# Two-layer decoder trunk with mixture-of-experts: Router's work area outside the weight ring, first gathers in the expert block, transposes of the next block at its end

## What is computed

```python
def hier_moe(h, w_rg, b_rg, w_re, b_re, w_gate, w_up, w_down):
    g_top = argmax(xf @ w_rg + b_rg)                 # one of 4 groups
    top_vals, top_idx = lax.top_k(chosen, 2)         # 2 of the 8 experts in it
    weights = p_g[:, None] * softmax(top_vals)
    # every token goes to its 2 of 32 experts:
    #   (silu(x @ w_gate[e]) * (x @ w_up[e])) @ w_down[e], weighted and summed
```

## Time and profile before

| | us |
|---|---|
| median of 3 runs | 1706.45 (1704.6 to 1708.78) |
| the profiled execution, device time | 1702.92 |
| its span, first to last instruction | 1700.7 |
| PE busy / DVE busy / ACT busy / POOL busy in the span | 1543.7 / 689.9 / 298.5 / 44.8 |
| mean granted TensorE clock | 0.968 |
| expert block of layer 0, about | 270 to 758 |
| expert block of layer 1, about | 1185 to 1700 |
| bytes read from HBM | 468.64 MB |

### The profile page before, as it was taken

One profiled execution on the slowest core, in us unless ns is written; L12 is line 12 of the kernel. 1 busy time (PEld: TensorE's weight loads), 2 busy tenths in 40 slices (PEclk: granted clock), 3 DMA queues, 4 the chain that ended last, 5 costly groups with the idle time before them and its releaser, 6 DMA issues. The chain is left out here.

```text
span 1700.7 us, 18753 instructions
## 1 busy us (share of the span) xinstructions
PE 1543.7 (91%) x7356; PEld 719.3 (42%) x7356; DVE 689.9 (41%) x1453; ACT 298.5 (18%) x648; POOL 44.8 (3%) x59
## 2 busy tenths in 40 slices
PE   7999985999998899959999899994999999898994
PEld 3444442444443334435554455552344444333342
DVE  3111353343333333346264587545233333323334
ACT  2000010000100000022243477511000000000001
POOL 0000000000000000000000000000000000000000
PEclk9999997999999999989999999997999999999997
DMA  6261227999999999935310300144999999999992
GB/s 198 74 256 66 78 100 308 420 421 421 421 420 420 422 421 419 419 132 154 98 51 0 149 1 1 19 171 169 418 421 421 419 421 422 421 420 421 420 417 93
DMA packets 109938, 465.28 MB, mean 274 GB/s; under 512 B 26512, under 2 KB 53136, under 8 KB 59920
## 3 DMA queue, kind: packets, MB, share of 16 engines
q1 hardware_dynamic: 104512, 455.56, 66.5%
q0 software_dynamic: 5328, 8.40, 1.4%
HBM read 468.64 MB, written 6.29 MB: 279 GB/s over the span
## 5 line engine op out<-in xcount | busy, mean ns | idle before, releaser
L832 PE MATMUL ps<-raw,e_xT 128*64 128x512 f32 x2080 | 470.9, 600 | 50.8 <-DMA raw<-in_expert_w_up 50.8
L832 PEld LDWEIGHTS ps<-raw,e_xT 128*64 128x64 f32 x2080 | 155.6, 138 | 354.6 <-issue 351.3
L856 PE MATMUL ps<-raw,e_hT 128*64 128x512 f32 x1040 | 237.5, 598 | 1.4
L963 DVE TENSOR_TENSOR e_sg_hid<-e_sg_hid,ps 64x512 f32<-64x512 f32 x65 | 44.2, 681 | 458.6 <-ACT e_sg_hid L905 458.6
L949 DVE TENSOR_TENSOR x_res<-x_res,ps 128x512 f32<-128x512 f32 x264 | 169.1, 682 | 12.2 <-PE ps L870 10.3
L366 PE MATMUL ps<-c_hT,raw 128*128 128x512 f32 x384 | 165.0, 592 | 0.2 <-ACT c_hT L311 0.2
L870 PE MATMUL ps<-e_yhi,e_pick 64*128 64x512 f32 x520 | 111.3, 423 | 13.1 <-issue 5.4
L856 PEld LDWEIGHTS ps<-raw,e_hT 128*64 128x64 f32 x1040 | 68.9, 136 | 128.0 <-issue 111.3
L905 ACT ACTIVATE e_sg_hid<-ps 64x512 f32<-64x512 f32 x65 | 38.6, 595 | 477.0 <-PE ps L832 477.0
L1530 PE MATMUL ps<-a_spare,raw 128*128 128x512 f32 x256 | 114.5, 604 | 1.5 <-DVE a_spare L1321 1.5
L913 ACT ACTIVATE e_yhi<-ps,e_wtab 128x512 fp32r<-128x512 f32 x65 | 44.8, 689 | 395.8 <-PE ps L856 395.8
(11 more groups left out here) (228 smaller groups left out, 1232.1 us busy)
## 6 DMA issues: line engine op xcount, KB each, us to landing
raw<-in_expert_w_gate SPq DMA_DIRECT2D x130, 1024.0 KB, 26.5
raw<-in_expert_w_up SPq DMA_DIRECT2D x130, 1024.0 KB, 27.2
raw<-in_expert_w_down SPq DMA_DIRECT2D x130, 1024.0 KB, 27.0
raw<-in_conv_w_in SPq DMA_DIRECT2D x12, 1024.0 KB, 9.8
raw<-in_w_kv SPq DMA_DIRECT2D x6, 1024.0 KB, 6.2
raw<-in_conv_w_out SPq DMA_DIRECT2D x1, 4096.0 KB, 19.0
rows_x<-raw SPq DMA_DIRECT2D x8, 512.0 KB, 2.7
raw<-in_attn_w_in SPq DMA_DIRECT2D x4, 1024.0 KB, 5.4
```

The source lines that it names most:

```text
L832: mm = pe.matmul(ps_gu[C - C * i:2 * C - C * i, :], xT[:, q % 2, k, u * C:(u + 1) * C], ring(m, L, p)[:, kk * F:(kk + 1) * F], start=(k == ...
L856: mm = pe.matmul(ps_y[n * C:(n + 1) * C, :], hT[:, 2 * h + kk, :], ring(m, L, p)[:, kk * D + n * 512:kk * D + (n + 1) * 512], start=(h == ...
```

## The change

- The ring gets a 17th place, `raw3`, in the expert block's own memory. `NR` is 17; the first 16 places are as before.
- `Router`'s work area no longer lies in ring places 8 to 11: its larger tiles (normed rows `xn`, now two tiles deep, and the turned features `hT`) go to a separate area (`c_hT` of the convolution in layer 0, an area of its own in layer 1), its small ones get memory of their own. Pieces 12 to 15 are therefore issued with 6 and 7 (layer 0) or with 2 to 7 (layer 1), ahead of the row writes, and the expert block issues piece 16 after the row writes have landed.
- With `xn` two tiles deep ACT waits in `squares` for the row write of the tile before last.
- The normed rows are written by ACT with the root alone; the gain is multiplied in at the eviction of the turned tokens in the expert block, so `gb`, a broadcast load of 512 KB, goes and a load of 4 KB (`gp`) comes.
- The first two gathers are issued by POOL at the head of the expert block, not in the mixer's block.
- The code tables `rhot`, `chot`, `ctok` and `cwts` share an area with the final norm's gain `gb`, whose load moves from the head of layer 1's expert block to behind the loads of chunk 2, after a wait on `s_wt`.
- In the overflow chunk the product goes to PSUM bank 5 and not 4, and its four token tiles all use the one pair of result banks; a tile waits for the adds of the one before it. DVE takes the overflow branch ahead of the last regular chunk's `dve_low`.
- In layer 0 PE does the 32 transposes for `shared_kv` at the end of the expert block, after all residual adds, each tile as soon as its rows are normed; `shared_kv` begins with their evictions and does not wait.

```diff
-NR = 16
+NR0 = 16
+NR = 17
...
-            prefetch(sp, m, 0, (6, 7))
+            prefetch(sp, m, 0, (6, 7, 12, 13, 14, 15))
...
+    def work(self, place):
+        half = NK * S // 2
+        self.xn = place[:, 0:half].rearrange("p (b d) -> p b d", b=2)
+        self.hT = place[:, half:2 * half].rearrange("p (b k q) -> p b k q", b=2, k=NK)
...
-        sp.dma_start(self.gb, a["norm_ffn"][L:L + 1, :].broadcast_to([P, D])).then_inc(self.s_gb, 16)
+            sp.dma_start(self.gp[:], a["norm_ffn"][L].rearrange("(p k) -> p k", k=NK)).then_inc(self.s_gb, 16)
...
         def squares(t):
             act.wait_ge(self.s_res, 2 * t + 2)
+            if t >= 2:
+                act.wait_ge(self.s_out[t % 2], 16 * (t // 2))
...
+        def normed(t):
+            act.wait_ge(self.s_root, t + 1)
+            act.activation(by_k_out(self.xn[:, t % 2, :]), by_k(m.x[:, t, :]), ACT.Copy,
+                           scale=m.rstd[:, self.n, t:t + 1]).then_inc(self.s_xn, 1)
...
-        pool.wait_ge(self.s_idx, 2)
-        pool.wait_ge(self.s_out, 16 * NT)
-        for q in range(2):
-            self.gather(pool, q)
...
         def pe_tile(pe, chunks, t, i):
-            wait(pe, s_add, 2 * (i - 1))
+            wait(pe, s_add, 2 * (i - 1) if i < LAST else 2 * i)
...
-            dve.tensor_copy(xT[:, q % 2, h * HK:(h + 1) * HK, :].rearrange("p k s -> p (k s)"), ps_t[:]
-                            ).then_inc(s_xev, 1)
+            if n == 0:
+                dve.wait_ge(r.s_gb, 16)
+            dve.tensor_tensor(xT[:, q % 2, h * HK:(h + 1) * HK, :], ps_t[:].rearrange("p (k s) -> p k s", k=HK),
+                              r.gp[:, h * HK:(h + 1) * HK].unsqueeze(2).broadcast_to([P, HK, GS]), ALU.mult
+                              ).then_inc(s_xev, 1)
...
-            sp.wait_ge(r.s_out, 16 * NT)
-            prefetch(sp, m, L, range(12, NR))
-            if L:
-                sp.dma_start(gb[:], m.a["norm_final"].rearrange("(a d) -> a d", a=1).broadcast_to([P, D])
-                             ).then_inc(s_gb, 16)
+            for s in r.s_out:
+                sp.wait_ge(s, 16 * (NT // 2))
+            prefetch(sp, m, L, range(NR0, NR))
             for c in range(E):
                 step(c)
+                if L and c == 2:
+                    sp.wait_ge(s_wt, 1)
+                    sp.dma_start(gb, m.a["norm_final"].rearrange("(a d) -> a d", a=1).broadcast_to([P, D])
+                                 ).then_inc(s_gb, 16)
...
         @block.gpsimd
         def _(pool):
+            pool.wait_ge(r.s_idx, 2)
+            for s in r.s_out:
+                pool.wait_ge(s, 16 * (NT // 2))
+            for q in range(2):
+                r.gather(pool, q)
...
+            overflow(dve, lambda c: dve_step(dve, c))
             dve_low(dve, E - 1)
-            overflow(dve, lambda c: dve_step(dve, c))
...
+            if L == 0:
+                pe.wait_ge(s_sum, 2 * NT)
+                nrm.tensor(pe, next_xn)
...
-            nrm.tensor(pe, xn, waiting=False)
...
-            prefetch(sp, m, 1, range(2, 8))
+            prefetch(sp, m, 1, (2, 3, 4, 5, 6, 7, 12, 13, 14, 15))
```

More of the change, by code:

```diff
@@ L126, in program @@
                 r = Router(nc, m, 0, layer, stage)
-                conv_mixer(nc, m, r, *right(nc, stage, ("c_hT", [P, NK, S], F32), ("c_u", [P, 2, S + 2], F32)),
-                           *[r.rows[:, i, :].rearrange("p (b s) -> p b s", b=2) for i in range(2)])
+                c = right(nc, stage, ("c_hT", [P, NK, S], F32), ("c_u", [P, 2, S + 2], F32))
+                r.work(c[0][:].rearrange("p k s -> p (k s)"))
+                conv_mixer(nc, m, r, *c, *[r.rows[:, i, :].rearrange("p (b s) -> p b s", b=2) for i in range(2)])
             experts(nc, m, 0, r)
@@ L434, in sem @@
             return m.sem(f"r{L}_{name}")
[L436 to L441, removed]
+        self.wr, self.bias, self.lg = sb(tmp, "wr", [P, NK, NL]), sb(tmp, "bias", [P, NL]), sb(tmp, "lg", [P, NL])
+        self.el, self.t32, self.falling = sb(tmp, "el", [P, E]), sb(tmp, "t32", [P, E]), sb(tmp, "falling", [P, E])
+        self.oh, self.slot = sb(tmp, "oh", [P, 2, NT, E]), sb(tmp, "slot", [P, NT, E])
+        self.late, self.gain = sb(tmp, "late", [P, NT, E]), sb(tmp, "gain", [P, NK])
+        self.gp = sb(keep, "gp", [P, NK])
         self.inc = sb(keep, "inc", [P, E])
@@ L574, in scalar @@
             squares(t)
+            normed(t)
         act.wait_ge(self.s_ge, 1)
@@ L655, in constants @@
         def constants():
-            own.step(dve.tensor_scalar(self.falling, m.iota[:, 0:E], -1.0, 64.0, ALU.mult, ALU.add))
+            own.step(dve.tensor_scalar(self.falling[:], m.iota[:, 0:E], -1.0, 64.0, ALU.mult, ALU.add))
             own.step(dve.memset(self.one[:], 1.0))
@@ L664, in scaled_weights @@
             dve.wait_ge(self.s_w, 80)
[L665 removed]
+            dve.tensor_tensor(self.wr[:], self.wr[:], self.gain[:].unsqueeze(2).broadcast_to([P, NK, NL]), ALU.mult
                               ).then_inc(self.s_wg, 1)
@@ L686, in slots @@
                                               op0=ALU.mult, op1=ALU.add))
[L687 removed]
+            own.step(dve.scalar_tensor_tensor(out=self.late[:], in0=rank, scalar=float(C) - 0.5, in1=each(begin),
                                               op0=ALU.is_gt, op1=ALU.mult))
[L689 to L690 removed]
+            own.step(dve.tensor_tensor(self.slot[:], rank, each(self.base[:, 0, :]), ALU.add))
+            own.step(dve.tensor_tensor(self.slot[:], self.slot[:], self.late[:], ALU.add))
             for k in range(2):
[L692 removed]
+                c = dve.tensor_tensor(self.oh[:, k], self.slot[:], self.oh[:, k], ALU.mult)
             own.step(c)
[L694 removed]
+            dve.tensor_reduce(m.slot[:].rearrange("p t k -> p k t"), self.oh[:], AX.X, ALU.add).then_inc(self.s_slots, 1)
             dve.wait_ge(self.s_slots, 1)
@@ L731, in vector @@
             root(t)
-            normed(t)
             if t < NT - 1:
@@ L799, in experts, with ps_y, low_done @@
         nrm = Norm(m, f"e{L}_next", 4 if L else 2)
+        next_xn = m.qr[:].rearrange("p k s -> p (k s)").rearrange("p (t d) -> p t d", t=NT)
         LAST = 4 * (E // PAIR - 1)
+        def ps_y(c):
+            return m.ps[4 if c < E else 5]
+        def low_done(eng, c):
+            if c < E:
+                wait(eng, s_ylo, c + 1)
+            else:
+                eng.wait_ge(s_olo, c - E + 1)
         def y_place(c):
@@ L849, in pe_down @@
             wait(pe, s_hev, c + 1)
-            wait(pe, s_ylo, c)
+            if c == E:
+                pe.wait_ge(s_add, 2 * LAST)
+            else:
+                low_done(pe, c - 1)
             for h in range(2):
```

96 lines of the change are left out of this document (39 added, 57 removed).

## The result

The changed kernel takes **1694.48 us** (median of 4 runs, 1693.45 to 1695.02) against 1705.53 for the kernel before (4 runs on the same chip), 11 us faster by the medians. The forecast was 1693.6 and "faster". The profiled execution took 1694.71 with a span of 1692.8; that of before took 1702.92 with 1700.7.

What follows compares the result with a forecast made beforehand. PE waits for weight pieces, so the DMA stream sets each expert loop's end. -7.0 - 5.5 - 3.6 + 3.3 = -12.8 us takes the profiled 1702.92 to 1690.1; against the median, 3.5 higher, 1693.6; range 1686 to 1701.

Steps and rivals of the forecast that it cites:

- Stream start, layer 0: Head of layer 0's expert loop: stream restarts 5.5 us later with five pieces less to carry, -7.0 us.
- 12.5 us less to carry: Layer 0's expert loop: five pieces already loaded when the stream restarts, 12.5 us of transfer saved.
- Layer 1: Layer 1's expert loop: the same gain as layer 0, less a 1.8 us hole at the `s_wt` wait, -5.5 us.
- Evictions: Eviction of turned tokens in the expert block: copying from PSUM becomes a product and costs nothing.
- End of layer 0: Seam to `shared_kv`: only eight transposes remain after the last norm, and DVE's branch goes first, -3.6 us.
- I give this 0.6: End of layer 0: DVE's overflow branch ahead of its last low part gains 0.6 us.
- I let these two cancel: End of layer 0: ACT and DVE starting together (up to 0.7 us) offsets PE's clock of 0.50 after idling.
- Overflow chunk: Layer 1's overflow chunk: one bank pair costs 0.85 us three times, plus a low part of 0.75, +3.3 us.
- (a): Rival, both expert loops: gathers land at 8.2 us, 3 us less gain per layer, 1699.7 us; chance 0.13.
- (b): Rival, both layers' barriers: something other than the gathers holds them, so +2.9 us, or +8.9 with slow landings; chance 0.05.
- (c): Rival, layer 1: row writes land late behind ten pieces and ACT waits; 13 us are spare; chance 0.01.
- (d): Rival: loop gains mostly lost in holes and clock, and the tail costs 5, -3, 1703 us; chance 0.06.

Runs made afterwards that it cites:

- again: The changed kernel once more with no edit: 1695.75 us, ratio 0.993 to the kernel before.
- late_pieces: The changed kernel with pieces 12 to 15 issued behind the barrier again, with piece 16: 1703.33 us, ratio 0.9984 to the kernel before.
- low_first: The changed kernel with the last chunk's low part ahead of VectorE's overflow branch again, in both layers: 1697.2 us.
- old_tail1: The changed kernel with layer 1's overflow chunk as in the kernel before (bank 4, alternating pairs, low part ahead of the branch): 1691.09 us.
- gathers_inside: The changed kernel with POOL issuing the first two gathers in the mixer's block again, as before: 1697.79 us.
- ring16: The changed kernel with 16 places in the ring instead of 17: 1695.82 us.
- best: The changed kernel with the gain loaded after all pieces, layer 1's overflow chunk as before, and piece 16 asked for after the second gather: 1684.00 us.
- after: The first profile of the changed kernel, no edit: profiled execution 1694.71 us.
- before: The kernel before the change, in its first profile: profiled execution 1702.92 us.
- turns_after: The changed kernel with the 32 transposes put back at the start of the next block, their waits restored: 1697.86 us.

## Why the prediction was right, and where it wasn't

**Stream start, layer 0 (-7.0 forecast).** A and B together: -6.0, the means of both profiles of each kernel. The barrier (262.0 forecast, 262.16 measured) and VectorE's 1.7 us (1.75) held. There are small misses. POOL issues at 263.04, the late end of what was allowed; the forecast counted from VectorE's last result at 263.37, but the index that the gather waits for was done at 262.90, so the kernel before had the same 0.9 us. The gate product starts at 270.91, not 270.3, and piece 17 follows it by 5.1 to 6.0 us, not 4.97: the granted clock came back from 0.50 to 1.00 some 2.8 us into that product in `again` and 4.7 in the first profile. The second profile of the kernel before has 5.5 us as well. "12.5 us less to carry" is sound as a sum but names the wrong benefit: `late_pieces` shows that four of the five pieces would have fitted into the wait for rows. The worth of loading them early is that they keep out of the gathers' way. The rows' landing is the link; the forecast had a price on it for piece 16, and none for the other four.

**Layer 1 (-5.5).** E gave -2.4 (479.8 against 482.2) and the earlier token list 1.7, which lies in D: -4.1. The hole was well sized (1.9 measured, 1.8 forecast). The failed term is the first gate product's start, 4.8 us earlier by "the same" as in layer 0: from the token list on it takes 9.54 to 9.68 us where the two profiles of before had 11.45 and 10.87, so with the 1.7 it is 2.9 to 3.6 earlier. About 1.0 of what it lacks is in the changed kernel, where the forecast had 8.6 us from token list to gate product (261.7 to 270.3) and POOL issued 0.8 us behind the barrier; the rest is that the kernel before was 0.3 to 0.9 us quicker there in layer 1 than in layer 0 (11.7), so "the same" had less to gain.

**Evictions (0).** L954 takes 0.69 us as a product of a PSUM operand and `gp`. Right.

**End of layer 0 (-3.6).** C gave -4.3 to -6.1. The step "I give this 0.6" for the branch ahead of the low part was too small: 1.7 (`low_first`). The transposes were worth 4.0 in C, 3.1 in the working. But "I let these two cancel" of the clock was wrong: ten profiles have both parts, the transposes and the branch first. In three of them the clock took 1.6 us back behind this stage, and in the other seven 1.1 to 1.3 within it and 3.1 to 3.3 behind it (last section).

**Overflow chunk (+3.3).** It cost 3.9, by `old_tail1`, near the forecast: the hand-overs take 0.82 to 1.31 instead of 0.85, and the low part, at 1671.91, costs nothing, since PE leaves its own branch only at 1674.26.

**Rivals.** (a) Gathers at 8.2 us: it is what `late_pieces` made of them (8.8 from issue to first transpose); beside one piece it was 4.9 to 5.3, as chosen. (b) falls by the barrier at 262.16. Its observation was a true one: a block's end waits some 3.2 us beyond POOL's last gather issue (264.59 to 267.79 in `gathers_inside`). The gathers explain it: the second lands 3.8 us after its issue at 263.59, at 267.4, and the barrier opens 0.4 later. (c) didn't occur: ACT has no wait for row writes. (d) is partly true, by the clock in D.

**The sum.** That 1693.6 was met within 0.9 is in part luck, since it is made of misses of both signs: +1.0 and +1.4 in the loops, -0.7 to -2.5 at layer 0's end, +0.6 in the tail, and D, which should have lost 1.7 and stands between -0.1 and +3.0. The gain is there (from the last tile's square on ACT to the token list it is 15.1 and 15.3 us, where the profiles of before have 16.8); the clock took it back (last section). The two spans of each kernel differ by 7.9 in their means (1701.55 and 1693.7), the medians by 11: the profiles of before lie below its median, and what its other executions spend isn't in any profile.

## What to carry to other kernels

Before you lengthen a prefetch, look at what else travels in the same stretch: here one load beside the critical gather made its rows 1.2 us later and four more another 3.9, and one wait ahead of the piece that wasn't urgent gave more in B and E (2.2 us) than the seventeenth place itself (0.9). A deeper ring pays only where the stream would otherwise run dry. Keep small loads that are needed late, and their own waits, off the queue that carries the stream: what stands behind them pays. If a change gives up an overlap in one stage for a gain in another, as with the bank pair, do it only in the layer that has the gain.

## What the runs showed of the hardware

**A gather and the pieces beside it.** From the first gather's issue to the first transpose of its rows: 3.7 to 3.9 us with no piece in the way (`ring16`, `best`), 4.9 with one, 8.8 with five (all layer 0). One gather's 512 KB and one piece take 1.25 and 2.49 us at 421 GB/s. Five pieces that begin at 262.2 can't be done before 274.6, and the rows were there at 271.83, so the gather doesn't stand behind all of them. Turns at equal shares, an assumption of mine, would add 1.25 in both cases; measured were +1.2 and +5.1 beside `ring16`. The Trainium skill ("DMA: Bandwidth & Descriptors", section SWDGE vs HWDGE vs iDMA) says that a DMA engine takes turns between the queues of GpSimd and SyncE. The first case agrees with this; the second is not explained by it, and its cause stays open.

**POOL's start.** Behind the barrier POOL needs 0.9 us until its first gather (262.16 to 263.04). Inside a block it needs the same behind the index: 0.94 us in `gathers_inside` (261.18 to 262.12) and 0.95 in the kernel before (262.90 to 263.85). The second gather follows 0.30 us behind the first's end. So it isn't the barrier that costs this time.

**ACT's write of normed rows.** It takes twice the time of the square over as many elements:

```profile
1153.08 1.06 ACT L561 ACTIVATE r_work<-x_res 128x1024 f32<-128x1024 f32 x1 [5.28 <-DVE x_res L605]
...
1155.47 2.13 ACT L574 ACTIVATE r_work<-x_res,rstd 128x1024 f32<-128x1024 f32 x1 [0.68 <-DVE rstd L615]
```

In the kernel before VectorE took 2.05 for it, so it may be the view that reorders the columns; that wasn't tried. The forecast's 1 us was wrong, and harmless.

**The clock at the seam of the layers.** These are busy time and granted clock (third number from the end) of the changed kernel in its two profiles, `after` first:

```profile
750.00:753.00 3.00, 2.13 (x19) 1.90 (x17) 0.70 (x1) 0.00 (x0) 0.00 (x0) 0.99 0.00 0
```

```profile
750.00:753.00 3.00, 2.58 (x16) 2.34 (x14) 0.05 (x1) 0.00 (x0) 0.00 (x0) 0.72 0.00 0
```

In both, TensorE had idled, was granted 0.50 (1.2 GHz) in the two us before 750 and got its 2.4 GHz back within the transposes; in `again` that came later, and the clock fell once more around the feature products (0.69 from 756 to 760). The transposes then took 6.33 us instead of 5.25, and D 415.6 instead of 413.2. Six other profiles have the same two lengths (6.3 to 6.6, and 415.5), two the short ones (5.2 to 5.3, and 413.2): 3.5 us for the same code.

Most of what D holds too much is the clock as well. The next rows run from the first feature product to SP's first issue behind the barrier before `attention`, in `before`, `after` and `again`:

```profile
766.16:948.95 182.79, 181.02 (x632) 94.84 (x632) 84.36 (x176) 54.95 (x93) 0.00 (x0) 0.98 0.23 71
```

```profile
754.97:939.41 184.44, 182.66 (x632) 96.16 (x632) 85.12 (x178) 54.69 (x93) 0.92 (x5) 0.97 0.24 72
```

```profile
755.41:941.35 185.94, 184.17 (x632) 97.04 (x632) 85.19 (x178) 54.80 (x93) 0.92 (x5) 0.96 0.24 71
```

The same 632 matmuls take 182.8, 184.4 and 185.9 us at a mean clock of 0.98, 0.97 and 0.96. All fourteen profiles fall into these three groups: both of before, `turns_after` and `low_first` into the first, `after`, `ring16` and `best` into the second, the seven with the long D into the third (185.9 to 186.1). So none of the ten profiles that have both parts of layer 0's new end reached the shortest time, and all four that lack one of them or both did. Why the clock falls more often behind the new end these profiles don't show, nor what puts a profile into the second group or the third: the code of that stretch is the same.
